# Fetching each expert's two weight rows by two half-size transfers into two rings

## The reference, cut to what matters

```python
sc = jnp.einsum('thpd,hpnd->thpn', q, sub_keys)            # 8 heads, 2 halves, 128 keys
top_v, top_i = lax.top_k(sc, 16)                           # per half
cand = top_v[:, :, 0, :, None] + top_v[:, :, 1, None, :]   # 256 pairs
best_v, best_pos = lax.top_k(cand, 16)
expert_id = jnp.take_along_axis(cand_id, best_pos, axis=-1)
gate = jax.nn.softmax(best_v, axis=-1)
u = jnp.take(u_table, eb, axis=0)                          # incoming weights
act = jax.nn.gelu(jnp.einsum('phkd,pd->phk', u, xb))
wgt = gb * act
out = jnp.einsum('phk,phkd->pd', wgt, jnp.take(v_table, eb, axis=0))   # outgoing weights
```

## Time and profile before

| | |
|---|---|
| median of 3 runs | 2862.39 us (2853.93 to 2864.79) |
| the profiled execution | 2854.61 us |
| its span, first to last instruction | 2852.9 us |
| mean granted TensorE clock | 0.953 of full |
| busy: PE, DVE, POOL, ACT | 84%, 58%, 52%, 24% of the span |
| HBM read | 639.00 MB |
| first row issued | 1527.37 us into the span |

### The profile page before, as it was taken

The page is one execution under the profiler, slowest core; times in us unless marked ns, Lnnn a source line. Parts: engine busy times, 40 slices in busy tenths (PEclk is TensorE's granted clock), DMA queues, the critical chain, the costliest instruction groups (busy, mean ns, idle before and its releaser), DMA issues. The chain is left out here.

```text
span 2852.9 us, 28061 instructions
## 1 busy us (share of the span) xinstructions
PE 2386.3 (84%) x9112; PEld 1544.5 (54%) x9112; DVE 1647.6 (58%) x3495; ACT 683.6 (24%) x1749; POOL 1469.4 (52%) x960
## 2 busy tenths in 40 slices
PE   8999689898989969679786888888877777777776
PEld 6888567787878739567664444444322322222222
DVE  1266695224523648640117788888778777555555
ACT  2111234214422220122412222222222222111112
POOL 6777355673367621366355665666544444344331
PEclk9999789998999979889998999999999999999999
DMA  3222001221122200022226999999999999999996
GB/s 131 95 96 96 1 1 60 81 90 44 46 81 89 88 1 1 8 67 96 89 87 249 420 421 421 420 415 419 420 421 422 422 421 421 422 421 421 422 422 264
DMA packets 103878, 642.63 MB, mean 225 GB/s; under 512 B 12624, under 2 KB 13008, under 8 KB 38096
## 3 DMA queue, kind: packets, MB, share of 16 engines
q0 software_dynamic: 73728, 536.90, 45.3%
q1 hardware_dynamic: 30032, 104.24, 10.9%
HBM read 639.00 MB, written 2.10 MB: 225 GB/s over the span
## 5 line engine op out<-in xcount | busy, mean ns | idle before, releaser
L2985 PE MATMUL bank<-peer_row,peer_diag 128*128 128x512 f32 x2048 | 961.4, 614 | 283.0 <-ACT peer_diag L2964 281.7
L2907 POOL DMA_INDIRECT peer_row<-in_peer_uv,peer_ids x512 | 579.4, 1132 | 658.3 <-PE bank L2985 617.6
L2985 PEld LDWEIGHTS bank<-peer_row,peer_diag 128*128 128x128 f32 x2048 | 376.3, 193 | 837.4 <-ACT peer_diag L2964 451.0
L2930 DVE CUSTOM_DVE_ANT_0 peer_row<-peer_row,peer_h_tok 128x1024 f32<-128x1024 f32 x512 | 641.5, 1257 | 322.6 <-DMA peer_row<-in_peer_uv,peer_ids 322.3
L206 POOL TENSOR_TENSOR w_parts<-ring,zero 128x1024 fp32r<-128x1024 f32 x152 | 288.4, 1897 | 282.5 <-PE bank L283 126.4
L209 POOL TENSOR_TENSOR w_parts<-ring,w_parts 128x1024 fp32r<-128x1024 f32 x152 | 369.7, 2432 | 27.6 <-POOL w_parts L206 27.6
L2964 ACT ACTIVATE peer_diag<-ident,peer_weight 128x128 f32<-128x128 f32 x512 | 177.4, 394 | 241.1 <-DVE peer_weight L2922 239.6
L2968 ACT ACTIVATE peer_acts<-peer_dots 128x2 f32<-128x2 f32 x256 | 52.1, 204 | 741.8 <-DVE peer_dots L2930 741.8
L259 PE MATMUL bank<-ssm_h_high,w_parts 128*128 128x512 f32 x512 | 159.1, 392 | 0.8 <-DVEq L642 0.8
L259 PEld LDWEIGHTS bank<-ssm_h_high,w_parts 128*128 128x128 f32 x512 | 97.0, 189 | 21.5 <-DVEq L642 1.0
L2682 PE MATMUL bank<-peer_h_high,w_parts 128*128 128x512 f32 x256 | 107.4, 469 | 0.0
(11 more groups left out here) (543 smaller groups left out, 3884.0 us busy)
## 6 DMA issues: line engine op xcount, KB each, us to landing
ring<-in_weights SPq DMA_DIRECT2D x180, 512.0 KB, 3.3
peer_row<-in_peer_uv,peer_ids POOLq DMA_INDIRECT x512, 24.2
resid<-in_x SPq DMA_DIRECT2D x1, 2048.0 KB, 7.5
out<-resid SPq DMA_DIRECT2D x4, 512.0 KB, 7.7
xa_mem<-in_mem SPq DMA_DIRECT2D x1, 1024.0 KB, 5.0
peer_gain<-in_rows SPq DMA_DIRECT2D x2, 512.0 KB, 6.4
peer_keys<-in_peer_keys SPq DMA_DIRECT2D x1, 1024.0 KB, 7.2
ssm_o_gain<-in_rows SPq DMA_DIRECT2D x1, 512.0 KB, 3.3
```

Source lines behind the costliest of these rows:

```text
L2907: pool.indirect_dma_start(self.rows[row][:, :], None, self.m.ins["peer_uv"], bass.IndirectOffsetOnAxis(ap=self.choice.ids[:, t, slot:slot ...
L2930: dot = dve.tensor_tensor_reduce(mine, mine, self.tokens(slot_of(j)[0]), 1.0, 0.0, ALU.mult, ALU.add, self.dots[:, h % 4, r:r + 1])
L2985: mm = pe.matmul(self.m.banks[2 * t + half][:, :], self.diag[:, j % (2 * GROUP), :], self.rows[row][:, D + half * 512:D + (half + 1) * 512 ...
```

## The change

The table `peer_uv` is taken apart into `peer_u` and `peer_v`. Each row j is now two indirect transfers of 4 KB per partition, both issued by POOL, u first. The u halves have a ring of their own with IN_ROWS = 6 buffers of 4 KB (`rows_in`), and v halves one with 12 buffers, then 20 (`rows`). The u buffer of row j-6 is free when the dots of its group are done (`dots_ready`), the v buffer as before by `row_used`, now that of row j-12, and of row j-20 from row 216 on. DVE waits for the u half alone. PE has a new wait, for the v half. The buffers take as much memory as before, 18 halves instead of 9 rows and 26 instead of 13. SWITCH is now 216, and the wait for `tokens_made`, whose gain tile lies where one buffer does, stands ahead of row 11 instead of row 3.

```diff
-FIRST_ROWS, ROWS, SWITCH = 9, 13, 207
+IN_ROWS, FIRST_ROWS, ROWS, SWITCH = 6, 12, 20, 216
...
-                if j == 3:
+                if j == FIRST_ROWS - 1:
                     pool.wait_ge(tokens_made, 2)
...
-        places = [58 + 8 * n for n in range(8)] + [8] + [H_AT + 8 * n for n in range(4)]
-        self.rows = [m.at(kb, f"peer_row{n}", [P, 2 * D]) for n, kb in enumerate(places)]
+        places = [58 + 4 * n for n in range(6)] + [86 + 4 * n for n in range(9)] + [8, 12, 82] + [H_AT + 4 * n for n in range(8)]
+        self.rows_in = [m.at(kb, f"peer_row_in{n}", [P, D]) for n, kb in enumerate(places[:IN_ROWS])]
+        self.rows = [m.at(kb, f"peer_row{n}", [P, D]) for n, kb in enumerate(places[IN_ROWS:])]
...
+        chosen = bass.IndirectOffsetOnAxis(ap=self.choice.ids[:, t, slot:slot + 1], axis=0)
         if j % TOPK == 0:
             pool.wait_ge(self.choice.ids_ready, self.choice.ready_for(j))
+        if j >= IN_ROWS:
+            pool.wait_ge(self.dots_ready, (j - IN_ROWS) // GROUP + 1)
+        pool.indirect_dma_start(self.rows_in[j % IN_ROWS][:, :], None, self.m.ins["peer_u"], chosen)\
+            .then_inc(self.loaded_in[j % IN_ROWS], 16)
         if slot_before(j) >= 0:
             pool.wait_ge(self.row_used, slot_before(j) + 1)
-        pool.indirect_dma_start(self.rows[row][:, :], None, self.m.ins["peer_uv"],
-                                bass.IndirectOffsetOnAxis(ap=self.choice.ids[:, t, slot:slot + 1], axis=0))\
+        pool.indirect_dma_start(self.rows[row][:, :], None, self.m.ins["peer_v"], chosen)\
             .then_inc(self.loaded[row], 16)
...
-                row, use = row_of(j)
-                dve.wait_ge(self.loaded[row], 16 * (use + 1))
-                mine = self.rows[row][:, 0:D]
+                dve.wait_ge(self.loaded_in[j % IN_ROWS], 16 * (j // IN_ROWS + 1))
+                mine = self.rows_in[j % IN_ROWS][:, :]
...
-            row, _ = row_of(j)
+            row, use = row_of(j)
             pe.wait_ge(self.diag_ready, j + 1)
+            pe.wait_ge(self.loaded[row], 16 * (use + 1))
...
-                               self.rows[row][:, D + half * 512:D + (half + 1) * 512],
+                               self.rows[row][:, half * 512:(half + 1) * 512],
```

More of the change, by code:

```diff
@@ L2881, in __init__ @@
         self.ends = last_groups()
+        self.loaded_in = [sem(f"peer_loaded_in{s}") for s in range(IN_ROWS)]
         self.loaded = [sem(f"peer_loaded{s}") for s in range(ROWS)]
@@ L3072, in lay_out @@
     arrays["peer_keys"] = a["peer_sub_keys_2"][0].reshape(HP, KEYS, P).transpose(2, 0, 1)
-    arrays["peer_uv"] = np.concatenate([a["peer_u_2"][0], a["peer_v_2"][0]], axis=1)
+    arrays["peer_u"] = np.ascontiguousarray(a["peer_u_2"][0])
+    arrays["peer_v"] = np.ascontiguousarray(a["peer_v_2"][0])
     arrays["x"] = a["x"].reshape(SEQ, D)
```

## The result

The changed kernel takes 3025.95 us (median of 4 runs, 3017.44 to 3034.39), the kernel before 2863.59 us (4 runs, 2853.93 to 2867.64). The ratio is **1.0568 [1.054, 1.0597]**, 162 us more. The forecast was 3080 us, slower with 0.95, range 2940 to 3200. The profiled execution took 3017.44 us against the 3079 of the sum: the direction and the cause came out as said, the size was 62 us too large.

The account below looks back on a forecast made before the run. Transfers bound the kernel before; POOL's issues would bind after. 1024 x 1.435 us plus 63.4 of splits from 1527.37 us end at 3060.2; less 2.6, plus 5.3, 14.5 and 1.7 gives 3079, stated as 3080 us, range 2940 to 3200.

Parts of the forecast that it names:

- the sum: Whole kernel: POOL's stage 1532.8 us after its first issue at 1527.37, plus the tail, giving 3079 us.
- What binds: Expert layer: transfers bind before at 421 GB/s; with two issues per row, 2.87 us at the mean, POOL sets the pace.
- Half a row costs a whole issue: POOL's row transfers: a half row has the same 144 packets per issue, so the whole price is taken.
- The mean of an issue, 1.132 us: POOL's 1024 issues: mean of the 512 before, with the gap 1.435 us each; ends 1.00 and 1.225 us.
- Gaps, splits, first issue: POOL's stage: about 0.303 us between issues, 12 exposed weight splits totalling 63.4 us, first issue at 1527.37 us.
- The tail: End of stage: less 2.6 us to the last u issue, plus 5.3 landing and 14.5 from last dot to span end.
- What would show it: Expert layer signs: POOL without gaps beyond 0.30 us, transfers at 350 to 365 GB/s, rows landing in 5 to 7 us.
- The new waits: PE's v-half wait is covered, at most 1.4 us once uncovered; POOL's `dots_ready` wait hides by 1.6 us.
- Rival 1: Expert layer: transfers stay the bound, 4 KB pieces making a row 2.53 us, +21.6 us, 2876 us; chance 0.10.
- Rivals 2 to 4: Shorter ends, 2841 us, chance 0.03; issues and dots in step, 3258 us, 0.06; u ring too short, 3259 us, 0.04.
- lockstep: POOL and DVE: each landing u starts a dot that holds one of two issues, 3.22 us a row, 3258 us; chance 0.06.
- the slack sum: u ring of six: row j-5 issued 14.4 us earlier against 12.8 us of landing, dots and DVE delay; 1.6 us slack.

Follow-up runs that it names:

- the tiny transfers: Kernel before, whole rows and one ring, plus a second indirect transfer of 64 bytes per partition for each row: 3029.38 us, ratio 1.0618.
- that queue thinned: Changed kernel with v transfers of 512 of 1024 columns, both matmuls using those, 134 MB less: 3096.16 us, ratio 1.0825.
- the experiment that should have shown it by itself: Changed kernel with its 12 weight splits in the stage working on 8 of 1024 columns, on chip C: 3051.39 us, ratio 1.0684.
- the holding gone: Changed kernel with DVE summing the u row alone, one SBUF input, instead of the dot product with the tokens: 2910.92 us, ratio 1.0177.
- the half-v run: Changed kernel with v transfers bringing 512 of 1024 columns and u and its dots unedited: 3096.16 us, ratio 1.0825.
- spaced issues: Changed kernel with half of v and no dot product, plus one 64-column POOL operation and a wait behind each issue pair, on D: 3069.34 us, ratio 1.0738.

## Why the prediction was right, and where it was off

- **What binds.** Right. POOL is without a gap over 0.3 us from the first issue to the last, and the tiny transfers show that the number of issues alone does it (3029 us on chip A, beside 3026 in the first runs).
- **Half a row costs a whole issue.** Right, and more so than said: 64 bytes cost the same. The reason given, the same 144 packets, was not the right one, since 32 packets cost as much; the price of a half row came out right with a wrong reason behind it. The Trainium skill (DMA: Bandwidth & Descriptors, "Anatomy of one DMA") puts a transfer's dispatch at some 50 ns and calls descriptor generation small. The issues of this kernel differ from that: at 0.94 + 0.30 us each they are what binds.
- **The mean of an issue, 1.132 us.** This is the step that failed: "I take the mean of all 512". It measured 1.070, inside the ends of 1.00 and 1.225. That is 63.5 us too much in the sum; the tail was 1.5 us too little, and the two make the miss of 62. The reason given for a lower value, that dots fill less of a longer row, is not what happened: 507 of 1024 issues began inside a dot, and 258 of 512 before, the same half. What fell is the part of the dot still to run, 0.40 us in the mean instead of 0.48. Most of it fell late: the last quarter of the issues, at 0.989 us, makes 37 of the 63.5 us. There the transfers were close to full (408 GB/s at 2.57 us a row) and the dots fell where they hold little; with that queue thinned the same kernel had 1.158. On chip D the same kernel took 3104 us, above the sum of 3079, by standstills for which the forecast had no term; that the sum lies nearer to this time is luck.
- **Gaps, splits, first issue.** 311 and 63.0 us against 310.3 and 63.4; 1527.20 against 1527.37. That a split is wholly exposed follows from POOL having no gap; the experiment that should have shown it by itself did not, because of the standstills.
- **The tail.** 18.7 us from the end of the last issue to the end of the span, 17.2 said. The last u issue began 2.2 us before that end (2.6 said) and its dot 6.6 us after that (5.3 said).

```profile
2994.75 0.99 POOL L2910 DMA_INDIRECT peer_row_in<-in_peer_u,peer_ids  x1 [0.31 <-issue]
...
2996.05 0.93 POOL L2914 DMA_INDIRECT peer_row<-in_peer_v,peer_ids  x1 [0.30 <-issue]
...
3001.32 1.23 DVE L2935 CUSTOM_DVE_ANT_0 peer_row_in<-peer_row_in,peer_h_tok 128x1024 f32<-128x1024 f32 x1 [1.30 <-DMA peer_row_in<-in_peer_u,peer_ids]
```

- **What would show it.** Transfers of 350 GB/s were said for the stretch with splits and 365 for late in the stage: 352 and 408 came, since issues took 1.02 us from 2500 to 2700 us and 0.98 from 2700 to 2900. Landing in 5 to 7 us: 6.4. The new waits cost nothing, as said.
- **Rival 1.** Its mechanism is there behind POOL: 410 GB/s with 4 KB pieces, 2.56 us a row where 2.53 was said. With the holding gone the kernel lands at 2911 us, not at 2876, because pieces, ring and splits come together.
- **Rivals 2 to 4.** No gain lay in the end (9 buffers); there was no lockstep, but its mild form is the half-v run; the u ring is no bound at six, and at four costs less than the slack sum had it.

What stays open: what the standstills on ACT, DVE and PE are, whether the recording of the trace has a part in them, and why chips C and D show them and A does not. They came only in kernels with 1024 issues, in the runs on those two chips, and shrank with spaced issues; on D, no kernel with 512 issues has a trace. Whether the spread lies in the chip, or in where and when a run was placed on it, was not told apart. No complete kernel here is faster than the one before. A kernel with two rings and one issue per row was not built.

## What to carry to other kernels

Cost an indirect transfer by its issue on POOL, here, for 128 rows, 0.94 us and a 0.30 us gap whatever its bytes: two per row need 2.48 us before anything holds them, and if the transfer of the row takes 2.49 there is no room. Before splitting a transfer to free a buffer earlier, take buffers away from the old kernel: if nothing is lost, as with 9 for 13 here, there is nothing to win. And once POOL is the bound, look at what DVE does when an issue begins, for two-input operations that were free before are then paid for. And if a trace lacks landings that it should have, do not read a cause from its missing releasers.

## What the runs showed of the hardware that was not expected

- An issue's length depends on the phase of DVE's dots: 1.197 us in the mean if it begins inside one, 0.946 if not. 134 MB fewer bytes made the kernel 70 us slower (on chip A, where the tiny-transfer kernel took as long as the changed one elsewhere), with issues of 1.158 us instead of 1.070.
- 0.94 us for an indirect issue of 128 pieces, the same for 64 bytes, 2 KB, 4 KB and 8 KB per piece, and for 32 packets as for 144.
- Standstills of up to 17 us on ACT, DVE and PE, on two chips and with 1024 issues only, in traces that lack 45 to 66% of the transfers' semaphore events; the changed kernel took 3026 us in the first runs and 3104 on chip D, where the kernel before differs by 0.3%.
